# Plain float32 projections in place of high and low parts, in a hybrid encoder layer with 32 experts

## The reference

```
h    = rmsnorm(x, g_mix);  proj = h @ w_in              # 1024 x 6680 columns: FoX q/k/v/forget, delta-net q/k/v/beta/decay/z, gates
y_a  = fox_attend(rmsnorm(fq), rmsnorm(fk), fv, ...)    # softmax attention with forget gates, 8 heads of 64
conv = silu(causal_conv([bq, bk, bv], w_conv))          # 2048 columns, width 4
y_b  = rmsnorm(gdn_chunked(cq, ck, cv, g, beta, s0)) * silu(bz)   # gated delta rule in chunks of 64, 8 heads
x1   = x + (sig(ga) * (y_a @ w_br_a) + sig(gb) * (y_b @ w_br_b)) @ w_out
x2   = x1 + hier_moe(rmsnorm(x1), w_grp, w_exp, w_e1, w_e3, w_e2) # each row goes to 2 of 32 experts,
                                                                  # silu(x @ w1) * (x @ w3) @ w2, 1024 -> 512 -> 1024
```

## Time and profile before

| | |
|---|---|
| three runs | 1338.45, 1338.7, 1349.24 us; median 1338.7 |
| the profiled execution | 1336.63 us |
| its span, first to last instruction | 1334.8 us |
| mean granted TensorE clock | 0.931 |
| PE busy in the span | 1116.3 us, 84% |
| DVE, ACT, POOL busy | 416.3, 359.2, 365.2 us |

### The profile page before, as it was taken

One profiled execution on the slowest core, in us unless ns is written; L12 is line 12 of the kernel. 1 busy time (PEld: TensorE's weight loads), 2 busy tenths in 40 slices (PEclk: granted clock), 3 DMA queues, 4 the chain that ended last, 5 costly groups with the idle time before them and its releaser, 6 DMA issues. The chain is left out here.

```text
span 1334.8 us, 20588 instructions
## 1 busy us (share of the span) xinstructions
PE 1116.3 (84%) x8278; PEld 855.8 (64%) x8278; DVE 416.3 (31%) x921; ACT 359.2 (27%) x743; POOL 365.2 (27%) x408
## 2 busy tenths in 40 slices
PE   3999899889997749999899866888888887777870
PEld 3999788779996748888898753444444444444440
DVE  5497623961111334442122461301111000010013
ACT  5447533342222744443332311000000000000000
POOL 2454559622222312122453012111212211111100
PEclk9999889889998969999999877899999999998996
DMA  6332236154324221114431966999999999999965
GB/s 119 80 80 64 73 83 159 43 152 125 88 52 141 79 81 48 48 48 132 125 88 45 385 266 219 386 367 405 412 398 417 411 406 411 399 407 410 406 281 204
DMA packets 149142, 285.06 MB, mean 214 GB/s; under 512 B 43858, under 2 KB 119218, under 8 KB 132688
## 3 DMA queue, kind: packets, MB, share of 16 engines
q1 hardware_dynamic: 94112, 243.76, 48.8%
q10 hardware_dynamic: 49216, 29.17, 7.9%
q0 software_dynamic: 5744, 11.16, 2.4%
HBM read 267.60 MB, written 24.31 MB: 219 GB/s over the span
## 5 line engine op out<-in xcount | busy, mean ns | idle before, releaser
L453 POOL TENSOR_TENSOR cv_w_lo<-cv_w_raw,cv_w_hi 128x1024 fp32r<-128x1024 f32 (+1 forms) x69 | 162.2, 2352 | 409.5 <-ACT cv_w_hi L446 409.1
L2373 PE MATMUL bank<-e_w,b_xT 128*64 128x256 f32 x2048 | 238.1, 390 | 42.7 <-DVE b_xT L2400 31.9
L467 PE MATMUL bank<-xhi,cv_w_hi 128*128 128x272 f32 x848 | 260.7, 307 | 10.5 <-POOL cv_w_lo L453 7.8
L467 PE MATMUL bank<-xhi,cv_w_lo 128*128 128x272 f32 x848 | 251.3, 296 | 0.0
L467 PE MATMUL bank<-xlo,cv_w_hi 128*128 128x272 f32 x848 | 250.8, 296 | 0.0
L2373 PEld LDWEIGHTS bank<-e_w,b_xT 128*64 128x64 f32 x2048 | 147.7, 141 | 123.0 <-DVE b_xT L2400 38.7
L467 PEld LDWEIGHTS bank<-xhi,cv_w_hi 128*128 128x128 f32 x848 | 166.3, 196 | 15.6 <-POOL cv_w_lo L453 9.6
L467 PEld LDWEIGHTS bank<-xlo,cv_w_hi 128*128 128x128 f32 x848 | 166.7, 197 | 1.2
L467 PEld LDWEIGHTS bank<-xhi,cv_w_lo 128*128 128x128 f32 x848 | 166.2, 196 | 0.0
L2385 PE MATMUL bank<-e_w,b_hiddenT 128*64 128x512 f32 x512 | 128.1, 646 | 28.5 <-DVE b_hiddenT L2407 15.2
L2351 POOL COPY b_target<-slot_target 128x1 int32 (+1 forms) x32 | 6.0, 187 | 372.9 <-ACT b_y L2395 365.1
(11 more groups left out here) (426 smaller groups left out, 1660.4 us busy)
## 6 DMA issues: line engine op xcount, KB each, us to landing
e_w<-in_w_e SPq DMA_DIRECT2D x96, 2048.0 KB, 35.3
cv_w_raw<-in_w_in ACTq DMA_DIRECT2D x33, 512.0 KB, 4.2
cv_w_raw<-in_w_in SPq DMA_DIRECT2D x19, 512.0 KB, 3.8
cv_w_raw<-in_w_br_b ACTq DMA_DIRECT2D x8, 512.0 KB, 3.8
o_raw<-in_w_out SPq DMA_DIRECT2D x16, 256.0 KB, 4.7
g_values_gates<-g_z_stage ACTq DMA_DIRECT2D x12, 272.0 KB, 4.7
f_gates<-g_values_gates SPq DMA_DIRECT2D x2, 1088.0 KB, 8.5
x_in<-in_x_prompt SPq DMA_DIRECT2D x4, 512.0 KB, 6.8
```

Of the source, the lines that this page charges most:

```text
L453: self.k.nc.gpsimd.tensor_tensor(self.wlo[:, s, 0:nk, :], self.raw[:, s, 0:nk, :], self.whi[:, c % OPS, 0:nk, :].bitcast(F32), ALU.subtract)\
L467: last = self.k.nc.tensor.matmul(self.bank(c, h)[:, 0:HALF], w, x[:, d, cols], start=(d == 0 and n == 0), stop=(d == nk - 1 and n == 2))
L2373: last = nc.tensor.matmul(k.bank[bank][sl[a], 0:FH], xT[:, d, :], w[slot][:, d, FH * a:FH * a + FH], start=(d == 0), stop=(d == KD - 1))
```

## The change

All projections become one plain float32 product of the loaded weight and the plain rows, for the three of high and low parts.

- `start`, `head_rows`, `fox_heads`: x is kept once (`xT`, by ACT), the delta-net output stays as it is (`yb`), the attention is kept once by ACT (`keep_out`). DVE's low parts and ACT's high parts of yb go.
- `Stream`: four slots of raw weights, no high or low slots; PE waits for the load itself. `ahead` only issues the load, four chunks on. Both splits are gone, so POOL only squares, solves, grows the state and zeroes.
- `mixed_rows`: the sum is written by tiles of rows (`mp`, `ms`, two ACT operations); all 16 loads of `w_out` are issued by SP at the stage's start, both halves have a place of their own.
- `project_and_choose`: SP issues router and expert loads with no `w_out` load ahead; w1 of the third expert is loaded at once (its place, in the late region, is free by the new layout), w3 after the fourth tile, w2 after the fifth. `idx` is made before the totals, and POOL issues the first three gathers at the end of this stage.
- `expert_blocks`: six blocks are unrolled (three before) and DVE's plan for the further blocks is spread over them; ACT's two exponentials come ahead of block 0. The final sum is joined: SP and ACT load the scattered rows when POOL has seen all of them stored (`all_in`), with no barrier; DVE sums in the same block.

The core of the diff:

```diff
-RAWS, OPS = 3, 3
-LEAD = OPS - 1
+RAWS = 4
@@ start
-                    nc.scalar.activation(k.xhi[:, 4 * b:4 * b + 4, c0:c0 + n],
+                    nc.scalar.activation(k.xT[:, 4 * b:4 * b + 4, c0:c0 + n],
...
-                    v.wait_ge(hi_done, 2 * t + b + 1)
-                    nc.vector.tensor_tensor(k.xlo[:, 4 * b:4 * b + 4, c0:c0 + n],
@@ Stream
     def ahead(self, a, c, h):
-        if h == 0 and c + LEAD < len(self.chunks):
-            self.split_hi(a, c + LEAD)
         if h == 1 and c + RAWS < len(self.chunks):
             self.load(a, c + RAWS)
...
     def part(self, pe, c, h, d):
         if d == 0:
-            pe.wait_ge(self.lo, c + 1)
+            pe.wait_ge(self.loaded[c % RAWS], self.loads_of(c))
...
-        for n, (w, x) in enumerate(((whi, xhi), (whi, xlo), (wlo, xhi))):
-            last = self.k.nc.tensor.matmul(self.bank(c, h)[:, 0:HALF], w, x[:, d, cols],
-                                           start=(d == 0 and n == 0), stop=(d == nk - 1 and n == 2))
+        last = self.k.nc.tensor.matmul(self.bank(c, h)[:, 0:HALF], self.w[:, c % RAWS, d, :],
+                                       self.k.rows[self.chunks[c][2]][:, d, h * HALF:(h + 1) * HALF],
+                                       start=(d == 0), stop=(d == nk - 1))
@@ head_rows
             for h in range(H):
                 gated(h)
-                if h >= 1:
-                    low(h - 1)
@@ mixed_rows
-            for j in range(4):
+            for j in range(KD):
                 o.load(sp, j)
...
-                nc.scalar.activation(mh[:, c, :], tmp[:, c % 2, :], ACT.Copy, scale=0.5).then_inc(high, 1)
+                nc.scalar.activation(mp[:, :, c, :], prompt(c), ACT.Copy, scale=0.5)
+                nc.scalar.activation(ms[:, c, :], tmp[:, c % 2, 0:NS], ACT.Copy, scale=0.5).then_inc(kept, 1)
@@ OutStream
+    def product(self, pe, bank, t, d, h):
+        k, n = self.k, TILES[t][1]
+        rows = k.ms[:, d, :] if t == 0 else k.mp[:, t - 1, d, :]
+        return k.nc.tensor.matmul(bank[0:n, :], rows, self.w[h][:, d, :], start=(d == 0), stop=(d == KD - 1))
@@ project_and_choose
-            for j in (2 * KD - 2, 2 * KD - 1):
-                o.load(sp, j)
...
+            load_weights(k, sp, "w_e1", k.w1, k.w1_loaded, RING - 1, RING - 1)
+            sp.wait_ge(projected, 4)
+            load_weights(k, sp, "w_e3", k.w3, k.w3_loaded, RING - 1, RING - 1)
             sp.wait_ge(projected, 5)
-            load_up(k, sp, RING - 1, RING - 1)
             load_down(k, sp, RING - 1, RING - 1)
...
+            g.wait_ge(tabulated, 1)
+            for b in range(RING):
+                g.indirect_dma_start(out=k.xg[:, b, :], out_offset=None, in_=k.table,
@@ expert_blocks
+                a.wait_ge(diffs, 1)
+                nc.scalar.activation(gd[:], gd[:], ACT.Exp).then_inc(exps, 1)
+                nc.scalar.activation(e2[:], e2[:], ACT.Exp).then_inc(exps, 1)
+                run_blocks(a, scalar_part)
+                load_rows(a, 1)
```

More of the change, by code:

```diff
@@ L388, in mixer_tensors @@
     k.yb = k.cv
+    k.rows["yb"] = k.yb
     k.smt = k.sb("small_rows", [128, 5, 96], F32, ctx)
@@ L495, in halves @@
         return [(c, h) for c, h, d in self.parts[name] if d == self.nk(c) - 1]
-    def splits(self, name):
-        return [c + LEAD for c, h in self.halves(name) if h == 0 and c + LEAD < self.n]
 def even(total, names):
@@ L1632, in _ @@
             norms.exps(a, 4, 4)
-            for h in range(4, H):
-                high(h)
 def fox_heads(k):
@@ L1665, in fox_heads @@
     with nc.Block() as block:
-        @block.gpsimd
-        def _(g):
-            for j in range(J + 2):
-                for x in "ab":
-                    for c in fill.splits(f"{x}{j}"):
-                        s_.split_lo(g, c)
         @block.tensor
@@ L1858, in _ @@
                 if j >= 2:
-                    high(j - 2)
+                    keep_out(j - 2)
                 if 1 <= j <= J:
@@ L1869, in mixed_rows @@
     nc, ctx = k.nc, k.stage
-    s_, mh, ml, part = k.first_stream, k.mh, k.ml, k.part
+    s_, mp, ms, part = k.first_stream, k.mp, k.ms, k.part
     ga, tmp = k.sb("m_gate", [128, 2, NT], F32, ctx), k.sb("m_sum", [128, 2, NT], F32, ctx)
-    gated, high, low = (k.sem("m_" + x) for x in ("sum", "high", "low"))
+    gated, kept = (k.sem("m_" + x) for x in ("sum", "kept"))
+    prompt = lambda c: tmp[:, c % 2, NS:].rearrange("p (t n) -> p t n", t=4)
     o = k.out_stream
@@ L1972, in split_lo @@
-    def split_lo(self, g, j):
-        g.wait_ge(self.hi, self.turn[j] + 1)
-        self.k.nc.gpsimd.tensor_tensor(self.wlo[:, j % KD, :], self.raw[:, j % KD, :], self.whi[:, j % KD, :].bitcast(F32),
-                                       ALU.subtract).then_inc(self.lo, 1)
-    def products(self, pe, bank, t, d, start):
-        k, c0 = self.k, TILES[t][0]
-        for i, (x, w) in enumerate(((k.mh, self.whi), (k.mh, self.wlo), (k.ml, self.whi))):
-            last = k.nc.tensor.matmul(bank[:], x[:, d, c0:c0 + 128], w[:, d, :], start=(start and i == 0),
-                                      stop=(d == KD - 1 and i == 2))
-        return last
+        self.w = [k.over(f"o_w{h}", [128, KD, 512], F32, "late", at) for h, at in ((0, 0), (1, 4 * KD * (512 + NT)))]
@@ L1984, in first_half @@
     def first_half(self, pe, d):
-        pe.wait_ge(self.lo, self.turn[d] + 1)
+        pe.wait_ge(self.loaded[d], 16)
         for t in range(5):
-            last = self.products(pe, self.k.bank[2 + t], t, d, d == 0)
-        last.then_inc(self.used, 1)
+            self.product(pe, self.k.bank[2 + t], t, d, 0)
     def second_half(self, pe, bank, t, first):
@@ L1994, in second_half @@
             if first:
-                pe.wait_ge(self.lo, self.turn[KD + d] + 1)
-            last = self.products(pe, bank, t, d, d == 0)
+                pe.wait_ge(self.loaded[KD + d], 16)
+            last = self.product(pe, bank, t, d, 1)
         return last
@@ L2417, in run_blocks @@
         def run_blocks(eng, part, beside=lambda s: None):
-            for s in range(RING):
-                part(eng, s, s, 0, s - RING)
-                beside(s)
-            with eng.Fori(1, STEPS) as i:
+            for b in range(EARLY):
+                part(eng, b, b % RING, b // RING, b - RING)
+                beside(b)
+            eng.wait_ge(planned, 1)
+            n = eng.value_load(k.nmore[0:1, 0:1], min_val=0, max_val=MORE)
+            with eng.Fori(EARLY // RING, STEPS) as i:
                 for s in range(RING):
@@ L2436, in _ @@
             def _(sp):
-                with sp.Fori(1, STEPS) as i:
+                for b in range(RING, 2 * EARLY):
+                    loads(sp, b, b, b % RING, b - RING)
+                sp.wait_ge(planned, 1)
+                n = sp.value_load(k.nmore[0:1, 0:1], min_val=0, max_val=MORE)
+                with sp.Fori(2 * EARLY // RING, STEPS) as i:
                     for s in range(RING):
```

315 lines of the change are left out of this document (84 added, 231 removed).

## The result

The changed kernel takes 1377.27 us (median of four runs, 1376.21 to 1379.12) where the one before takes 1338.58: a ratio of 1.028, 95% interval 1.0229 to 1.0331. The forecast was 1378. The profiled execution, 1379.12 us, has a span of 1377.3 us, 42.5 more than before. Two executions in all took far longer than every other, 2487.66 us of the kernel before beside the first experiments and 4201.96 us of the kernel with only the exponentials as before, and no time given here rests on them.

The account below looks back on a forecast made before the run. PE's own work was taken to bound the kernel nearly everywhere, expert weight loads from 890 us on. Stage terms summed to +40.5, so 1377, taken as 1378 us; own range 1358 to 1396, stated range 1352 to 1402.

Parts of the forecast that it names:

- The price of a part: In the projections, a plain float32 part costs 458 ns, 80 more than its three float32r passes; 1040 parts, +83 us.
- Rival B: All projections: plain records issue as fast as float32r's, 126 ns, so a part is 252 for 378; 1240 us; chance 0.04.
- The reliefs of `convolved_projections` and `delta_net`: Idle time and clock give back 6.4 and 1.7 us, then 5 and 9, leaving the stages at +15 and +10.
- Rivals A and C: Added PE time: A, it only fills waits and keeps the clock up, 1350, chance 0.12; C, relief doesn't arrive, 1400, 0.08.
- `mixed_rows`: In this stage, 192 parts +15.4 and 40 products +6.8, with 4.7 us of idle time given back: +17.5 us.
- The burst of `w_out` loads: In `mixed_rows`, SP's 16 loads, 4 MB at once, go past the chunk loads: costed at nothing, 3 if cover fails.
- The start: Before the first projection, PE's longest wait for POOL's low part, 7.8 us, falls: -4 us, bounds -7.8 and -1.
- `head_rows`: In this stage, dropped low parts -3.5 and ACT's high parts -2.6, with 2.4 of longer PE parts let through: -3.7 us.
- The project stage: In `project_and_choose`, 40 products cost +6.8 us and 2.2 come back from clock and idle time: +4.6.
- Early gathers: Before the first expert block, POOL's gathers start right after `idx`, not after the barrier: a gain of 1.4 us.
- The second block: In `expert_blocks`, PE's 6.96 us wait goes with exponentials ahead and the plan spread; weights start earlier: -7 us.
- The end: From POOL's last operation to the first load of the rows, barrier and stage entry go: -6 us.

Follow-up runs that it names:

- the two-pass kernel: Kernel before with the third float32r pass left out of the parts and of w_out's products (reduced precision): 1266.8 us, one execution.
- the two kernels with float32r projections: Kernel before with the change's end, three-pass projections kept: first three gathers early, 1326.57 us, or issued after the barrier, 1326.65 us.

## Why the prediction was right

**The price of a part.** Right: 229 ns a record, 458 a part, in 53 distances where the forecast had three, and 2080 records. With 512 columns 429 ns, forecast 431. Rival B is out.

**Where it lands.** Right by stage within 3 us, as the table shows. That the total is within 1 us is luck on top: the terms miss by up to 2.8 us in either direction, and `delta_net` alone scatters by more.

The reliefs of `convolved_projections` and `delta_net`, 8 and 14 forecast, were 9 and 13. The main cause is shown: cover by longer work, with the splits kept; in `delta_net` some 3 us of it hang on the splits. How `delta_net`'s 14 were made up was not right: 5 of idle time and 9 of the clock were given back, and it was 9.6 of idle time and 3.0 of busy time, with the clock at 0.94 for 0.91. Two errors of opposite sign left the sum near. `convolved_projections` had 6.4 and 1.7, and 6.7 and 2.1 came, though its 11.1 us of idle time were counted from 26.5; from the first projection at 30.1 there were only 7.5, and the difference is the wait that the start had already been credited with. The granted clock is 0.98 in both kernels there. DVE's operations did get shorter with the splits gone, but DVE was not last, and `delta_net` came out at +12 and not at +3. By the Trainium skill ("SBUF — State Buffer", Who interferes with whom), VectorE and GpSimd exclude each other at a shared port pair; the DVE times agree with it (504 to 507 ns free of POOL's work, up to 2356 beside it), and it says nothing of who is last. Rivals A and C, both about this relief, each lie one side of it.

**`mixed_rows`**, +20.3 for +17.5. The waits did go: idle time fell from 5.1 to 1.1 us, 4.0 for the 4.7 forecast. The term that was mis-sized is the price of the products: the narrow sample tile, which the forecast costed like the others, took 2.5 us more. The burst of `w_out` loads did nothing: PE is busy 125.1 of 126.2.

**The start**, -1.7 for -4: the transposes' own chain and the barrier were nearer behind than the middle of the bounds.

**`head_rows`**, -5.3 for -3.7: the removed operations brought 7.1 (forecast 6.1), and PE's longer parts cost 1.8 (forecast 2.4). DVE's last chain is 6.2 us, 498.77 to 504.96, for 9.9: -3.7 where -3.5 was forecast. One reading was wrong. PE's wait of 15.4 us before `fox_heads`, which the prediction said "stays", is 9.6 now. It is PE standing at the barrier until that chain of DVE has ended (486.04, with PE going on at 486.90), so it is the same time seen from PE, and it shrinks with the chain. It was costed at no change, so the sum did not suffer.

**The project stage**, to the index table +2.4 us (67.8 for 65.4) where +4.6 was forecast. Its 40 products cost 6.7 us more if their records stand 429 ns apart, as measured in one group; the relief is then 4.3 for 2.2. PE's busy time up to the table grew by 4.1 us and the clock went from 0.83 to 0.88. Which of them gives the relief was not tried.

**Early gathers.** The step "with three gathers before the barrier I give it 1.4" was wrong in sign: against gathers behind the barrier they cost 2.6 us. It was compared with the kernel before, where a barrier, a copy of the index and a wait stood in the path; against that, 8.2 us are now 7.8, and with the gathers behind the barrier they are 5.2. The copy stood in the path for 1.2 us before (797.50 to 798.69); how much of the 3.0 between 8.2 and 5.2 it explains wasn't tried, and on the old projections the gathers behind the barrier, also without the copy, took 8.75.

**The second block.** Right in place and nearly in size: -8.8 for -7, and +8.4 when undone. The check given for it was off: the DMA share over the first 70 us of the blocks is 0.89 for 0.78 before, not 0.85 for 0.76, counted from the first block:

```profile
859.80:929.80 70.00, 60.40 (x443) 33.68 (x445) 17.51 (x57) 7.11 (x13) 12.37 (x27) 0.95 0.89 354
```

**The end.** -6.1 for -6.

**Rival B's sum** had a flaw that the two-pass kernel shows: it let `convolved_projections` gain 30 us where it gains 3.5. Its total was near by luck, as the middle stages gave 37 for 15. DVE's 96 us of busy time was read as the floor of that stage. In fact PE waits there for ACT (8.9 and 6.3 us), for DVE (4.4 and 1.2) and, after the first chunk, for POOL's low parts (5.3), at a clock of 0.86, and that holds the stage at 125.

**The range.** "Combined as independent errors" the stated bounds give about 1365 to 1395; the 1358 of the forecast's own range is lower than they do.

What stays open is the 3.3 us of the project stage, up to the index table, between the two kernels with float32r projections: their clocks differ, and why the clock falls in one of two like stretches wasn't tried. `delta_net` has the same scatter: 264.1 to 271.7 us among five kernels that don't differ in it.

## What to carry to other kernels

Count passes by the distance between their starts, from a long stretch of the same type and width, before trading several cheap ones for one dear one: here three float32r passes are 378 ns and one plain product 458. Removing work from engines that wait is worth something only at the places where their chain is last; find these, and keep that part of a change. Here the end of the change alone, on the old projections, is the fastest version of full precision: 1326.6 us, 0.7% under the kernel before and 3.7% under the changed one. Work moved ahead of a barrier delays everyone behind it, by as much as the engine that does it arrives later than the rest.

## What was not expected of the hardware

- A stationary operand of 32 columns between ones of 128 makes the products dearer, not cheaper: 490 ns a record for 430, and the next ones later too, 2.5 us over 16 records in eight groups.
- A DVE operation with one tensor and a scalar column (128x547) takes 505 ns with POOL idle, and up to 2356 when one of POOL's subtractions (2352 ns on average in the kernel before) is under way: it ends after the subtraction. The one with two tensors takes 790 ns undisturbed, and up to 2994 in the kernel before beside POOL's work. Their means, 1157 and 937 in one kernel, 1186 and 1260 in another, only say how often the two met.
- Adding 23 us of PE work to a stage costs 14, and taking 36 away brings 3.5. PE's idle time goes the other way: 0.8 us with the longer parts, 7.5 before, 28.7 with the shorter; and so does, with the shorter, the granted clock (0.98, 0.98 and 0.86).
